# Two transformer blocks on one core: the low part of each weight half made in two GpSimd instructions of 512 elements instead of one of 1024

## The chip, the cores and the metric

The kernel runs on one core of one Trainium2 chip. Its time is the device time of one execution in microseconds (us). The engines of the core are TensorE (PE in the rows; its weight loads are PEld), VectorE (DVE), ScalarE (ACT), GpSimd (POOL) and SyncE (SP), which here only issues transfers.

## The reference, cut to what matters

Two blocks run one after the other on 256 tokens of width 2048, in float32. Nearly all of the work is the product of an activation with a large weight matrix:

```python
x = first_block(x, c, w_ada, ..., w_in, ..., w_out, ..., w_up, ..., w_down, final_norm_g)
return second_block(x, mem_2, ..., w_in_2, ..., w_xq_2, w_xk_2, w_xv_2, w_xo_2, ..., w_gate_2, w_up_2, w_down_2, final_norm_2)

# first_block
mod = jax.nn.silu(c) @ w_ada[l] + b_ada[l]            # 2048 -> 12288
h = rms_norm(x, norm_mix_g[l]) * (1.0 + scale_m) + shift_m
proj = h @ w_in[l]                                     # then block attention and a state space mixer
mix = jnp.concatenate([attn, ssm], axis=-1) @ w_out[l]
x = x + gate_m * mix
x = x + gate_f * conv_ffn(h, w_up[l], conv_ffn_w[l], conv_ffn_b[l], w_down[l])   # 2048 -> 11264 -> 2048

# second_block: neighbourhood and latent attention, attention on a memory, then
def swiglu(h, w_gate, w_up, w_down):
    return (jax.nn.silu(h @ w_gate) * (h @ w_up)) @ w_down
```

## The kernel before, in words

**Two parts of every weight.** TensorE takes operands of the type float32r. A float32 weight is therefore split in two: its high part `w_hi` is the weight cast to float32r, and its low part `w_lo` is the weight less that high part. The activation is split likewise into `a_hi` and `a_lo`. A product is three matmuls into the same sum: high by high (L1102), low activation by high weight (L1104), and high activation by low weight (L1106). Where the weights are the moving operand, the three stand at L1116, L1118 and L1120.

**The stream.** All weights pass in one fixed order (the list `STREAM`) as 442 tiles of 128 x 2048 elements, 1 MB each. A tile has two halves of 128 x 1024. A half `h` passes four engines:

- SyncE loads its tile into one of four slots of `raw` (`stream_tile`, L405). Before it overwrites a slot, it waits until the low parts of the old tile are made, since those read `raw`.
- ScalarE casts the half into `w_hi[h % 4]` (`hi`, L515). It first waits for `half_used`, which says that TensorE has finished half `h - 4`.
- GpSimd subtracts and writes `w_lo[h % 4]` (`low_part`, L481 to L485, the instruction at L484). It waits for `hi_ready` of the half and signals `lo_pool`. It does so for 882 of the 884 halves; the two halves of the tile `dt` are made by VectorE. GpSimd does nothing else but a few fills at the start.
- TensorE waits for `lo_pool` once ahead of a half (`wait_half`) and then runs its matmuls: 8 products of three matmuls of 256 columns (`half_T`), or 4 products of three of 512 columns (`half_N`, for the weights `xv`, the last third of `qkv` and a few others). Then it signals `half_used`.

So there are four slots of high and low parts: ScalarE and GpSimd can be up to four halves ahead of TensorE.

**Around the stream.** The stages come in this order: `xk`, `xv` (the keys and values of the memory for the second block, put first), `xs`, `dt`, `bz`, `qkv`, `wb`, `wa`, `up`, `down` for the first block, then `win2`, `uq`, `ukv`, `wa2`, `wb2`, `xq`, `xo`, `gu`, `down2` for the second. The heads of the attentions and of the mixer are worked between halves.

**The modulation.** The product with `w_ada` runs beside the stream on VectorE. 192 rows of 128 x 1024 are loaded into a ring of four slots, later two (`ada_row` in the SyncE program), and each is multiplied by an element of a vector and added to a sum (L1711; in the `up` stage L2144). Such an instruction reads two operands from on-chip memory. SyncE's queue holds tiles and rows in one order: `tiles_beside` puts about one row behind each half in the early stages. A row that waits for its slot (`ada_used`) holds back the tiles behind it.

**VectorE's other work** is the norms (L1792, L1801), the low parts of the activations (L1784, L1861, L2216), residuals, and the convolution behind `up` (L1875, L1880).

In every program, the order is that in which the code is written; no scheduler changes it.

Of the kernel before, what the change touches and what calls it, by code (L numbers as in the profile page):

```python
# [23 lines left out]
F32 = mybir.dt.float32  # L24
F32R = mybir.dt.float32r
I32 = mybir.dt.int32
ALU = mybir.AluOpType
# [11 lines left out]
HALF = TILE // 2  # L39
RAW = 4  # L40
SLOTS = 4
# [151 lines left out]
def block_program(nc, stream, ada, xT, memT, vecs, consts, onehot, relb, rpb, out, rel_dram,  # L193
                  rpb_dram, k_dram, v_dram):
    ctx = ExitStack()
    with ctx:
        def sb(name, shape, dt=F32):
            return ctx.enter_context(nc.sbuf_tensor(name, shape, dt))

        def sem(name):  # L200
            return ctx.enter_context(nc.semaphore(name))
# [3 lines left out]
        w_hi = sb("w_hi", [P, SLOTS, HALF], F32R)  # L205
        w_lo = sb("w_lo", [P, SLOTS, HALF], F32R)
# [111 lines left out]
        hi_ready, lo_dve, lo_pool = sem("hi_ready"), sem("lo_dve"), sem("lo_pool")  # L318
# [69 lines left out]
        def raw_half(h):  # L388

            return raw[:, h // 2 % RAW, h % 2 * HALF:(h % 2 + 1) * HALF]  # L390
# [86 lines left out]
        @block.gpsimd  # L477
        def _(pool):
            pool.memset(ones[:, :], 1.0).then_inc(ones_ready, 1)

            def low_part(h, i=None, step=0):  # L481

                pool.wait_ge(hi_ready, h + 1 if i is None else i * step + (h + 1))
                pool.tensor_tensor(w_lo[:, h % SLOTS], raw_half(h), w_hi[:, h % SLOTS].bitcast(F32),  # L484
                                   ALU.subtract).then_inc(lo_pool, 1)  # L485

            def low_parts(name, a, b):

                h0, period = H0[name], 16
                n = (b - a) // period  # L490
                if n >= 2:
                    with pool.Fori(0, n) as i:
                        for h in range(h0 + a, h0 + a + period):
                            if not ON_DVE[h]:
                                low_part(h, i, period)
                    a += n * period
                for h in range(h0 + a, h0 + b):
                    if not ON_DVE[h]:
                        low_part(h)

            for name, n in STREAM:
                low_parts(name, 0, 2 * n)
# [2145 lines left out]
```

## Time and profile before

| what | us |
|---|---|
| median of 3 runs | 3088.03 (3085.39 to 3088.13) |
| the profiled execution | 3092.41 |
| its span, first to last instruction | 3090.6 |
| TensorE busy (matmuls) | 2819.7 |
| GpSimd busy | 2240.9 |
| VectorE busy | 1189.6 |
| ScalarE busy | 1178.4 |

The span is the time between the first and the last instruction in the trace; 1.8 us of the profiled execution lie around it. Busy time counts an instruction from its start to its end in the records, waiting for a shared resource included. TensorE's matmuls overlap in the records, so that its busy time says when it has work rather than how fast it does it.

### The profile page before, as it was taken

The page shows a single profiled execution, that of the slowest core. Times are in us where ns is not written, and L with a number is a line of the kernel's source. Part 1 is how long each engine was busy: PE and PEld are TensorE (multiplying, and loading weights), DVE is VectorE, ACT ScalarE, POOL GpSimd, SP SyncE. Part 2 cuts the span into 40 slices and gives each one's busy share as a digit, 9 for nine tenths or more (in the row PEclk, how much of TensorE's full clock was granted, in tenths as well). Part 3 has the DMA queues.
Part 4 walks back from the last instruction along what each step waited for, and adds up shares of the span by engine and source line. Part 5 has one row for each costly group of instructions (what it writes and reads, how often), then busy time and mean ns, then how long its engine had stood idle before and what let it go on. Part 6 is the DMA issues. An engine that isn't in the chain of part 4 may idle for free.

```text
span 3090.6 us, 51906 instructions
## 1 busy us (share of the span) xinstructions
PE 2819.7 (91%) x21456; PEld 2730.9 (88%) x21456; DVE 1189.6 (38%) x1334; ACT 1178.4 (38%) x1349; POOL 2240.9 (73%) x887
## 2 busy tenths in 40 slices
PE   4688988786789999999999997999999999999997
PEld 4676987675679999999999996799999999999997
DVE  4787765543643544522233525361121000001233
ACT  2333332223233333333455434353354333333442
POOL 2679584443458889887888975476688888887885
PEclk8889898988889999999999999999999999999998
DMA  7877465544436666554444554253455455554542
GB/s 218 337 299 294 183 248 207 202 176 179 181 125 224 226 224 235 221 179 163 178 175 177 191 186 128 95 200 143 150 177 182 184 178 188 177 184 163 183 179 93
DMA packets 111622, 589.78 MB, mean 191 GB/s; under 512 B 23276, under 2 KB 25324, under 8 KB 54796
## 3 DMA queue, kind: packets, MB, share of 16 engines
q1 hardware_dynamic: 92736, 570.84, 50.6%
q10 hardware_dynamic: 18764, 17.20, 2.2%
q8 instruction: 90, 1.47, 0.2%
q14 instruction: 32, 0.26, 0.0%
HBM read 577.79 MB, written 10.21 MB: 190 GB/s over the span
## 4 chain that ended last, share of the span: by engine, by line
PE 41%; POOL 28%; issue 23%; DVE 5%; DMA 2%; ACT 1%; POOLq 0%; ACTq 0%; SPq 0%; DVEq 0%
POOL w_lo L484 28%; PE ps L1102 12%; PE ps L1104 12%; PE ps L1106 12%; DMA arena<-ada 2%; ACT w_hi L515 1%; DVE arena L1711 1%; PE ps L1116 0%; PE ps L1118 0%; PE ps L1120 0%; DVE work L1801 0%; PE ps L1567 0%; DVE work L1792 0%; PE ps L1161 0%; PE ps L1536 0%
## 5 line engine op out<-in xcount | busy, mean ns | idle before, releaser
L484 POOL TENSOR_TENSOR w_lo<-raw,w_hi 128x1024 fp32r<-128x1024 f32 x882 | 2240.5, 2558 | 816.0 <-ACT w_hi L515 814.3
L1102 PE MATMUL ps<-a_hi,w_hi 128*128 128x256 f32 x6512 | 1872.5, 288 | 122.6 <-POOL w_lo L484 43.9
L1104 PE MATMUL ps<-a_lo,w_hi 128*128 128x256 f32 x6512 | 1859.1, 285 | 0.0
L1106 PE MATMUL ps<-a_hi,w_lo 128*128 128x256 f32 x6512 | 1858.1, 285 | 0.0
L515 ACT CAST w_hi<-raw 128x1024 fp32r<-128x1024 f32 x884 | 919.7, 1047 | 1322.4 <-PE ps L1106 1169.2
L1102 PEld LDWEIGHTS ps<-a_hi,w_hi 128*128 128x128 f32 x6512 | 1268.5, 195 | 131.8 <-issue 57.1
L1104 PEld LDWEIGHTS ps<-a_lo,w_hi 128*128 128x128 f32 x6512 | 1268.2, 195 | 0.6
L1106 PEld LDWEIGHTS ps<-a_hi,w_lo 128*128 128x128 f32 x6512 | 1266.7, 195 | 0.0
L1711 DVE SCALAR_TENSOR_TENSOR arena<-arena,small 128x1024 f32<-128x1024 f32 x150 | 325.7, 2201 | 245.4 <-DMA arena<-ada 244.7
L1861 DVE TENSOR_TENSOR a_lo<-arena,a_hi 128x1024 fp32r<-128x1024 f32 x44 | 107.2, 2441 | 348.3 <-ACT a_hi L781 348.3
L2488 DVE TENSOR_TENSOR work<-ps,rstd 128x512 f32<-128x512 f32 x22 | 15.2, 692 | 430.4 <-PE ps L1106 430.4
L1875 DVE TENSOR_SCALAR work<-ps,vec 128x256 f32<-128x256 f32 x100 | 47.5, 539 | 239.5 <-PE ps L1106 239.5
L1116 PE MATMUL ps<-w_hi,a_hi 128*128 128x512 f32 x264 | 111.5, 422 | 5.4 <-POOL w_lo L484 5.3
L1118 PE MATMUL ps<-w_hi,a_lo 128*128 128x512 f32 x264 | 106.1, 402 | 0.0
L1120 PE MATMUL ps<-w_lo,a_hi 128*128 128x512 f32 x264 | 105.9, 401 | 0.0
L2144 DVE SCALAR_TENSOR_TENSOR arena<-arena,small 128x1024 f32<-128x1024 f32 x32 | 84.3, 2657 | 44.5 <-DMA arena<-ada 44.0
L1880 DVE SCALAR_TENSOR_TENSOR work<-ps,vec,work 128x255 f32<-128x255 f32 (+2 forms) x212 | 87.7, 476 | 5.5 <-DVE work L1875 2.4
L1116 PEld LDWEIGHTS ps<-w_hi,a_hi 128*128 128x128 f32 x264 | 51.9, 197 | 23.3 <-POOL w_lo L484 10.8
L1120 PEld LDWEIGHTS ps<-w_lo,a_hi 128*128 128x128 f32 x264 | 51.4, 195 | 11.7
L1118 PEld LDWEIGHTS ps<-w_hi,a_lo 128*128 128x128 f32 x264 | 51.8, 196 | 10.0
L2239 DVE TENSOR_TENSOR arena<-ps,rstd 128x1024 f32<-128x1024 f32 (+1 forms) x15 | 18.1, 1205 | 108.7 <-PE ps L1106 108.6
L2206 DVE TENSOR_REDUCE stage_v<-work 128x256 f32<-128x1024 f32 (+1 forms) x18 | 35.0, 1954 | 54.8 <-ACT work L818 54.8
(209 smaller groups left out, 1264.5 us busy)
## 6 DMA issues: line engine op xcount, KB each, us to landing
raw<-stream SPq DMA_DIRECT2D x442, 1024.0 KB, 4.8
arena<-ada SPq DMA_DIRECT2D x192, 512.0 KB, 5.7
arena<-memT SPq DMA_DIRECT2D x4, 512.0 KB, 7.8
res<-xT SPq DMA_DIRECT2D x1, 2048.0 KB, 23.9
rel_rows<-arena ACTq DMA_DIRECT2D x1, 2048.0 KB
k_spill<-arena ACTq DMA_DIRECT2D x4, 512.0 KB, 7.0
v_spill<-arena ACTq DMA_DIRECT2D x4, 512.0 KB, 3.3
work<-rel_rows ACTq DMA_DIRECT2D x16, 128.0 KB, 2.2
```

What stands on the lines that cost most here:

```text
L484: pool.tensor_tensor(w_lo[:, h % SLOTS], raw_half(h), w_hi[:, h % SLOTS].bitcast(F32), ALU.subtract).then_inc(lo_pool, 1)
L515: act.copy(w_hi[:, base % 4], raw[:, tile_slot, (base % 2) * HALF:(base % 2 + 1) * HALF]).then_inc(hi_ready, 1)
L1102: pe.matmul(o, w_hi[:, h % SLOTS, w], a_hi[:, c0 + k, :], start=first and k == 0 and f % 2 == 0, stop=False, skip_group_check=True)
L1104: pe.matmul(o, w_hi[:, h % SLOTS, w], a_lo[:, c0 + k, :], start=False, stop=False, skip_group_check=True)
L1106: mm = pe.matmul(o, w_lo[:, h % SLOTS, w], a_hi[:, c0 + k, :], start=False, stop=last and k == 1, skip_group_check=True)
L1116: pe.matmul(out2[:, t, 0:width], a_hi[:, c0 + k, a], w_hi[:, h % SLOTS, w], start=first and k == 0, stop=False, skip_group_check=True)
L1118: pe.matmul(out2[:, t, 0:width], a_lo[:, c0 + k, a], w_hi[:, h % SLOTS, w], start=False, stop=False, skip_group_check=True)
L1120: mm = pe.matmul(out2[:, t, 0:width], a_hi[:, c0 + k, a], w_lo[:, h % SLOTS, w], start=False, stop=last and k == 1, skip_group_check=True)
L1711: ins = dve.scalar_tensor_tensor(out=a, in0=ada_slot(n % ring), scalar=ck, in1=a, op0=ALU.mult, op1=ALU.add)
L1861: dve.tensor_tensor(a_lo[:, a:a + 4, :], hidden[:, 4 * quad:4 * quad + 4, :], a_hi[:, a:a + 4, :].bitcast(F32), ALU.subtract).then_inc(hl_ ...
L1880: ins = dve.scalar_tensor_tensor(out=dst[:, c, shift:S], in0=src[:, c, 0:S - shift], scalar=w(c, taps - 1 - shift), in1=dst[:, c, shift:S] ...
L2144: dve.scalar_tensor_tensor(out=a, in0=ada_slot(s % 2), scalar=small[:, bass.ds(i * 2 + (16 + s // 2), 1)], in1=a, op0=ALU.mult, op1=ALU.ad ...
```

## The change

For each half, GpSimd makes the low part in two instructions, of the first and of the last 512 elements of each partition. It waits once, ahead of the first, for `hi_ready`, and signals `lo_pool` once, behind the second. So each of TensorE's and SyncE's waits stands for the same event as before: the whole half is made. The number of elements is the same. There are 1764 such instructions in place of 882. No other engine's program is changed. In the changed file the lines behind the edit are numbered higher by 2.

```diff
             def low_part(h, i=None, step=0):
 
                 pool.wait_ge(hi_ready, h + 1 if i is None else i * step + (h + 1))
-                pool.tensor_tensor(w_lo[:, h % SLOTS], raw_half(h), w_hi[:, h % SLOTS].bitcast(F32),
-                                   ALU.subtract).then_inc(lo_pool, 1)
+                for cols in (slice(0, HALF // 2), slice(HALF // 2, HALF)):
+                    ins = pool.tensor_tensor(w_lo[:, h % SLOTS, cols], raw_half(h)[:, cols],
+                                             w_hi[:, h % SLOTS, cols].bitcast(F32), ALU.subtract)
+                ins.then_inc(lo_pool, 1)
```

## Rows read from the trace of the kernel before

**Rows 1.** The page: busy us (share of span) and instructions of each engine.

```profile
PE 2819.7 (91%) x21456; PEld 2730.9 (88%) x21456; DVE 1189.6 (38%) x1334; ACT 1178.4 (38%) x1349; POOL 2240.9 (73%) x887
```

**Rows 2.** Windows, whole core: start:end, length, busy (count) by engine, clock, DMA.

```profile
199.00:303.00 104.00, 97.97 (x419) 75.52 (x418) 85.18 (x38) 37.86 (x37) 99.93 (x33) 0.98 0.83 310
...
910.00:1419.00 509.00, 508.99 (x4231) 509.00 (x4231) 219.34 (x325) 194.64 (x198) 436.65 (x174) 1.00 0.58 211
...
2295.00:2804.00 509.00, 508.50 (x4232) 508.09 (x4230) 41.23 (x59) 200.32 (x204) 426.00 (x177) 1.00 0.51 182
```

**Rows 3.** Timeline of GpSimd: start us, us, what, [idle before <- releaser].

```profile
15.51 9.27 POOL L484 TENSOR_TENSOR w_lo<-raw,w_hi 128x1024 fp32r<-128x1024 f32 x4 [14.56 <-ACT w_hi L515]
...
2499.39 2.41 POOL L484 TENSOR_TENSOR w_lo<-raw,w_hi 128x1024 fp32r<-128x1024 f32 x1 [0.47 <-ACT w_hi L515]
2502.27 2.41 POOL L484 TENSOR_TENSOR w_lo<-raw,w_hi 128x1024 fp32r<-128x1024 f32 x1 [0.47 <-ACT w_hi L515]
```

**Rows 4.** Windows by 100 us, whole core (columns as in rows 2).

```profile
1000.00:1100.00 100.00, 100.00 (x836) 100.00 (x835) 48.60 (x68) 37.38 (x38) 89.25 (x36) 1.00 0.62 229
```

**Rows 5.** Timeline of GpSimd and VectorE around the stage xv.

```profile
194.81 99.33 POOL L484 TENSOR_TENSOR w_lo<-raw,w_hi 128x1024 fp32r<-128x1024 f32 x32 [0.48 <-ACT w_hi L515]
...
198.69 60.14 DVE L1711 SCALAR_TENSOR_TENSOR arena<-arena,small 128x1024 f32<-128x1024 f32 x18
```

**Rows 6.** Timeline of TensorE in xv, three matmuls of a product in a row.

```profile
202.62 0.39 PE L1116 MATMUL ps<-w_hi,a_hi 128*128 128x512 f32 x1
202.85 0.39 PE L1118 MATMUL ps<-w_hi,a_lo 128*128 128x512 f32 x1
203.08 0.39 PE L1120 MATMUL ps<-w_lo,a_hi 128*128 128x512 f32 x1
```

**Rows 7.** Chain of waits, 199 to 303 us: start us, us, what.

```profile
264.38 1.00 POOL w_lo L484
265.37 2.33 issue
267.71 1.00 POOL w_lo L484
```

**Rows 8.** Waits in the whole span: who <- whom: us, times, longest.

```profile
PEld ps L1102 <- POOL w_lo L484: 46.8, 13, 27.5
PE ps L1102 <- POOL w_lo L484: 43.9, 10, 27.3
```

**Rows 9.** Timeline of GpSimd at the start: its other instructions.

```profile
0.25 0.10 POOL L2638 MEMSET const-float32-0.0<- 128x1 f32 x1 [0.25 <-issue]
0.29 0.10 POOL L2638 MEMSET const-float32-1.0<- 128x1 f32 x1
...
0.75 0.20 POOL L479 MEMSET ones<- 128x128 f32 x1 [0.29 <-POOLq L2638]
```

**Rows 10.** Chain of waits in the whole span: start us, us, what.

```profile
298.55 7.52 DVE work L1801 x4
...
337.08 3.42 DVE arena L1711
...
403.44 3.14 DVE arena L1711
...
790.62 3.47 DVE arena L1711
```

**Rows 11.** Timeline of VectorE behind 296 us.

```profile
298.55 7.51 DVE L1801 TENSOR_SCALAR work<-work,mod 128x256 f32<-128x256 f32 x4
...
309.06 1.14 DVE L1801 TENSOR_SCALAR work<-work,mod 128x256 f32<-128x256 f32 x4
```

**Rows 12.** The page: chain that ended last, its largest shares by engine and line.

```profile
PE 41%; POOL 28%; issue 23%; DVE 5%; DMA 2%; ACT 1%; POOLq 0%; ACTq 0%; SPq 0%; DVEq 0%
POOL w_lo L484 28%; PE ps L1102 12%; PE ps L1104 12%; PE ps L1106 12%; DMA arena<-ada 2%; ACT w_hi L515 1%; DVE arena L1711 1%; PE ps L1116 0%; PE ps L1118 0%; PE ps L1120 0%; DVE work L1801 0%; PE ps L1567 0%; DVE work L1792 0%; PE ps L1161 0%; PE ps L1536 0%
```

**Rows 13.** The page: DMA issues, KB each, us to landing.

```profile
arena<-ada SPq DMA_DIRECT2D x192, 512.0 KB, 5.7
```

**Rows 14.** The page: groups; count | busy us, mean ns | idle before.

```profile
L1711 DVE SCALAR_TENSOR_TENSOR arena<-arena,small 128x1024 f32<-128x1024 f32 x150 | 325.7, 2201 | 245.4 <-DMA arena<-ada 244.7
```

## The prediction, on record before the changed kernel ran

> **What bounds the kernel now.** I read the engines' totals first [rows 1]: TensorE is busy for 91% of the span, GpSimd for 73%, the other two for 38%. That makes TensorE the usual bound and GpSimd the second engine. But the change touches GpSimd alone, and a share over the whole span says nothing of the stages in which GpSimd comes last. So I went through the stages by windows [rows 2].
>
> In `gu` (2295 to 2804 us) TensorE has work all the time, and 176 halves take 509 us, 2.89 us each. GpSimd makes a low part in 2.41 us and then idles for 0.47 us until ScalarE's next cast [rows 3], which itself waits for TensorE to free a slot. An instruction may grow by up to 0.47 us per half there at no cost. `up` (910 to 1419 us) has the same pitch. Its first part is tighter: GpSimd is busy for 89.25 us of 100 [rows 4], so the 34.7 halves of 2.88 us in it leave 10.75 / 34.7 = 0.31 us each.
>
> `xv` (199 to 303 us) is another case: GpSimd is busy for 99.93 of 104 us [rows 2], with 32 instructions on end in 99.33 us [rows 5], 3.10 us each. TensorE needs less: three matmuls start 0.23 us apart [rows 6], and a half has twelve, 2.76 us. The chain shows the same pitch of 3.34 us again and again, 1.00 on GpSimd's instruction and 2.33 on TensorE's issue behind it [rows 7]. GpSimd sets the time of this stage.
>
> Why does an instruction take 3.34 us there when four on end at the start take 9.27 us, 2.32 each [rows 3]? Beside it VectorE runs rows of the modulation, 18 on end in 60.14 us, also 3.34 us each [rows 5]. The two engines take turns: 2.30 us for GpSimd and 1.04 us for VectorE, one after the other. In the Trainium skill, "SBUF — State Buffer" (on-chip memory), the part on the shared port pair, VectorE with two inputs there and GpSimd exclude each other for a whole instruction; by that rule, the trace agrees, the turn and not the element is the grain, and halving GpSimd's instruction halves VectorE's wait for its turn without changing the sum of a turn of each.
>
> Outside `xv`, TensorE waits for a low part 10 times ahead of L1102, 43.9 us in all, of which 27.3 is one wait near the start [rows 8]. These are the places where work other than the stream held TensorE or ScalarE up, and the next halves are then made as fast as GpSimd can.
>
> **What the change does, part by part.**
>
> *It adds 882 instructions.* Each half still has 1024 elements per partition, so the added cost is what an instruction costs beyond its elements; call it X, when the next one is ready behind it. The trace has no 512-element subtraction, so X is bounded by rows. From below: the tiny fills of one element follow each other 0.04 us apart (0.25 to 0.29) [rows 9]. A gain in GpSimd's own work is excluded, since no element is saved. From above: such a fill takes 0.10 us from start to end [rows 9] and has one operand where the subtraction has three; three such parts are 0.30 us (an estimate). The fill of 128 elements takes 0.20 us, so its elements cost 0.10 and the rest is again 0.10. I take X = 0.15 us, between 0.10 and 0.20, since a two-input instruction has more to start and to drain than a fill, but part of that overlaps: the instruction behind an idle gap takes 2.41 us, those on end 2.32 each, so about 0.1 us of an instruction's cost is already hidden when one follows another [rows 3].
>
> The Trainium skill, "GPSIMD Engine Reference", section 3.1, has 4497 ns for a subtraction-like instruction of 2048 elements. With this trace's 2.41 us for 1024, a line through both has 0.32 us beyond the elements, 0.22 when they run on end; by it X would be 0.22 and the cost below 16 instead of 11 us.
>
> *In `xv`* GpSimd is the bound, and X is paid for each of about 32 halves: 32 x 0.15 = 4.8 us.
>
> *At the 10 waits outside `xv`* TensorE waits for the next low part and then runs close behind GpSimd. At most four halves are in the ring, and I charge four per wait: 10 x 4 x 0.15 = 6.0 us. Some waits expose only one half and some a longer catch-up, so this is a rough term.
>
> *In the long steady stages* (`up`, `down`, `win2`, `xo`, `gu`, `down2`) the idle time of 0.47 us per half, or 0.31 us in the first part of `up`, hides X. Cost 0. The cover is gone above X = 0.31: then about 150 halves of `up` pay the excess.
>
> *Semaphores.* TensorE and SyncE wait for the whole half as before, so nothing starts earlier for having the first 512 elements. Gain 0. SyncE's tile load waits for the low parts too, but loads up to eight halves ahead of TensorE. Cost 0 beyond the X counted.
>
> *VectorE gets its turn sooner.* A VectorE instruction that finds GpSimd on the shared memory waits up to 2.30 us now and up to 1.15 us after. This counts only where VectorE is last. The chain has four long places of that kind [rows 10]. Three are single modulation rows of 3.42, 3.14 and 3.47 us, against 1.04 us in its turn; each can lose 1.15 us, 3.4 in all. The fourth is the norm behind `xv`: four L1801 take 7.51 us at 298.55 and only 1.14 us at 309.06 with nothing in the way [rows 11]. It waited behind nearly three GpSimd instructions, 6.4 us; behind as many of half the length it would be 3.2 us. Together 6.6 us. GpSimd loses what VectorE takes, and TensorE needs both, so I count 5 us of it as gained.
>
> *Sum:* 4.8 + 6.0 - 5 = +6 us (5.8). The profiled execution took 3092.41 us (span 3090.6, 1.8 around it) and would become 3098. It was 4.4 us above the median of the runs, 3088.03, so for the runs I predict 3094.
>
> **Rivals.**
>
> *A. The instruction is dear.* If X is 0.30 us, `xv` costs 9.6 and the waits 12.0; less 5, that is +17: 3105 us. At 0.35 the `up` stage joins with 150 x 0.04 = 6 us, and the sum is 11.2 + 14 + 6 - 5 = +26: 3114 us. For it: the subtraction has two inputs and an output to set up. Against it: 0.10 us for the shortest fill.
>
> *B. The instruction is almost free, and VectorE gains nothing.* With X at 0.04, `xv` costs 1.3 and the waits 1.6 us; the turns of VectorE move work around without shortening the chain. +3: 3091 us, no change. For it: GpSimd and VectorE need the same sum of turns. Against it: the 6.4 us in front of L1801 stand in the chain.
>
> *C. The shorter turn wins: faster.* Place: the modulation rows beside the stream from 300 to 860 us. Transfers of such rows make 2% of the chain, 62 us [rows 12]; at 5.7 us to the landing of one [rows 13] these are about 11, and each is released by a VectorE row that gave its slot free. SyncE's queue holds the weight tiles behind these rows, so 1.15 us sooner per row would bring tiles sooner: 11 x 1.15 = 13 us, plus 3.2 at the norm, 16 in all. Half of it, 8, against a cost of 3 at X = 0.04 gives -5 to -6 us: 3082; all of it 3075. It decides when X is below about 0.1 us. Against it: VectorE mostly waits for the transfer itself, not for GpSimd.
>
> *D. The steady stages lose their cover* though X is small, because GpSimd now meets VectorE twice per half: each of the two instructions may have to give VectorE a turn of 1.04 us. In `up` VectorE is busy 48.6 of 100 us [rows 4], its waits for turns included, and its rows come once per four halves, so a second turn per half is rarely asked for. Would it cost 0.1 us per half, X would be 0.25 in effect and the sum 8 + 10 - 5 = +13: 3101. I count it with A.
>
> **How the numbers follow.** The forecast, X from 0.1 to 0.2 and some of the turns gained, has a chance of 0.45; its own range is 3088 to 3101. A and D together have 0.22, B has 0.15, C has 0.18. A change of less than 0.2%, 6.2 us, can't be told from none. The forecast lies on that line, so 0.22 of its chance is slower and 0.23 is the same. A and D are slower (0.22), B is the same (0.15), and of C 0.14 is faster and 0.04 is the same. Slower 0.44, same 0.42, faster 0.14. The range is 3080 to 3116: it leaves out C in full and X above 0.35 us.
>
> **What would show it.** In the changed profile GpSimd has twice as many subtractions. In `gu` two on end should take about 2.41 + 0.15 = 2.56 us, with the idle time per half down from 0.47 to 0.32 us and the stage still at 509 us. In `xv` the pitch of a half should be near 3.34 + 0.15 where rows run beside it, and the stage some 5 us longer. VectorE's L1711 should fall from 2.20 us on average [rows 14] towards 1.6, and the four L1801 from 7.5 towards 4.3 us. The prediction is wrong in its cost if the two instructions on end take 2.35 or 2.75 us, and in its gain if L1711 gets shorter while the stages up to 900 us stay as long as they were, or shrink by more than 6 us.

## The result and the profile after

The changed kernel takes 3109.25 us (3107.62 to 3110.53, 4 runs) against 3088.08: 21 us slower, ratio 1.007 with a 95% interval of 1.0053 to 1.0088. Run again beside the experiments, on another chip, it took 3105.81 us against 3090.33, ratio 1.0046 (1.0033 to 1.006). So the cost is 14 to 21 us; forecast were 6, with a range from 8 us less to 28 more.

The engines' totals of the changed kernel (busy us, share, instructions), as [rows 1]:

```profile
PE 2828.5 (91%) x21456; PEld 2738.1 (88%) x21456; DVE 1041.8 (34%) x1334; ACT 1182.2 (38%) x1349; POOL 2402.4 (77%) x1769
```

GpSimd is busy for 161.5 us more; 882 x 0.15 would be 132, and the rest fits more waiting for its turn. VectorE is busy for 148 us less with the same instructions: it waits less for its turn.

GpSimd's timeline, at the start and in `gu`, as [rows 3]:

```profile
15.57 9.84 POOL L485 TENSOR_TENSOR w_lo<-raw,w_hi 128x512 fp32r<-128x512 f32 x8 [14.61 <-ACT w_hi L517]
...
2502.97 2.56 POOL L485 TENSOR_TENSOR w_lo<-raw,w_hi 128x512 fp32r<-128x512 f32 x2 [0.32 <-ACT w_hi L517]
2505.86 2.56 POOL L485 TENSOR_TENSOR w_lo<-raw,w_hi 128x512 fp32r<-128x512 f32 x2 [0.33 <-ACT w_hi L517]
```

Four halves on end take 9.84 us instead of 9.27, and a half in `gu` 2.56 instead of 2.41, with an idle time of 0.32 instead of 0.47. The price of the second instruction is 0.14 to 0.15 us, as forecast.

The groups of VectorE's modulation rows and of the activation's low parts, as [rows 14] (L1713 is L1711 of before; L1863 was L1861, 2441 ns on average):

```profile
L1713 DVE SCALAR_TENSOR_TENSOR arena<-arena,small 128x1024 f32<-128x1024 f32 x150 | 258.5, 1745 | 321.2 <-DMA arena<-ada 320.9
L1863 DVE TENSOR_TENSOR a_lo<-arena,a_hi 128x1024 fp32r<-128x1024 f32 x44 | 71.1, 1619 | 390.5 <-ACT a_hi L783 390.5
```

Where did the time go? This table has the end of each stage, read from the timeline as the end of the matmul that signals the stage's last half, in us, and how much later than before each profile is at that point. "Again" is the second run of the changed kernel; the last four columns are kernels of the experiments below:

| end of | before | changed | again | 16, 1008 | 1008, 16 | only xk | wait per piece |
|---|---|---|---|---|---|---|---|
| xk | 199.4 | -8.5 | -9.2 | -10.3 | -9.0 | -9.3 | -8.9 |
| xv | 302.4 | -1.3 | -3.8 | -2.6 | -3.0 | -7.7 | -4.8 |
| wa | 888.3 | +3.9 | 0.0 | -5.2 | +1.3 | -11.5 | +3.7 |
| up | 1418.6 | +6.6 | +2.7 | -4.7 | +6.0 | -8.8 | +3.6 |
| down | 1686.8 | +11.2 | +7.2 | -2.8 | +8.4 | -8.2 | +4.0 |
| win2 | 1890.2 | +16.7 | +12.3 | -1.1 | +10.2 | -8.1 | +6.6 |
| xo | 2294.9 | +17.7 | +14.0 | -0.3 | +14.6 | -7.1 | +3.6 |
| down2 | 3065.3 | +17.8 | +14.0 | -0.5 | +14.6 | -7.2 | +3.6 |

Each column is a single execution. That of the cut 16, 1008 was the fastest of its 11 (3091.89 us, median 3098.29), so its column is some 6 us too good as a whole; single stages can be compared. `gu` and `down2`, 770 us, lose nothing. `xk` gains 9 us, and what lies between loses more than forecast. Waits between 100 and 200 us, first of the kernel before, then of the changed one (who waited for whom: us, times, longest):

```profile
POOL w_lo L484 <- ACT w_hi L515: 29.6, 13, 17.1
...
PE ps L1186 <- DVE arena L1711: 7.8, 1, 7.8
```

```profile
POOL w_lo L485 <- ACT w_hi L517: 8.2, 2, 5.0
DVE arena L1713 <- DMA arena<-ada: 30.0, 13, 8.1
```

In `xk` TensorE stood for 7.8 us waiting for the 32 rows of the first modulation sum. With shorter turns VectorE has them ready in time: the changed kernel's list has no such wait. Then `xv` takes 110 us instead of 103 (108.5 in the second run). Not all of this is the price: with two pieces in `xk` alone, `xv` takes 104.5.

### The profile page after: what moved, and what is told of

Its sections match the earlier page's. It is cut to its first block, busy times and chain, and to the rows that moved or that the text cites. A ratio compares the mean times of both kernels' runs of the same rounds, so it can differ in the third digit from the quotient of the medians.

```text
span 3108.4 us, 52788 instructions
## 1 busy us (share of the span) xinstructions
PE 2828.5 (91%) x21456; PEld 2738.1 (88%) x21456; DVE 1041.8 (34%) x1334; ACT 1182.2 (38%) x1349; POOL 2402.4 (77%) x1769
## 4 chain that ended last, share of the span: by engine, by line
PE 39%; POOL 35%; issue 18%; DVE 4%; DMA 2%; ACT 1%; POOLq 0%; ACTq 0%; SPq 0%; DVEq 0%
POOL w_lo L485 35%; PE ps L1104 12%; PE ps L1106 11%; PE ps L1108 11%; DMA arena<-ada 2%; PE ps L1118 1%; PE ps L1120 1%; PE ps L1122 1%; PE ps L1569 0%; ACT w_hi L517 0%; PE ps L1425 0%; DVE rstd L2275 0%; PE ps L1538 0%; DVE arena L1713 0%; PE ps L1537 0%
## 5 line engine op out<-in xcount | busy, mean ns | idle before, releaser
L485 POOL TENSOR_TENSOR w_lo<-raw,w_hi 128x512 fp32r<-128x512 f32 x1764 | 2402.0, 1393 | 672.5 <-ACT w_hi L517 669.2
L1713 DVE SCALAR_TENSOR_TENSOR arena<-arena,small 128x1024 f32<-128x1024 f32 x150 | 258.5, 1745 | 321.2 <-DMA arena<-ada 320.9
L1863 DVE TENSOR_TENSOR a_lo<-arena,a_hi 128x1024 fp32r<-128x1024 f32 x44 | 71.1, 1619 | 390.5 <-ACT a_hi L783 390.5
L2146 DVE SCALAR_TENSOR_TENSOR arena<-arena,small 128x1024 f32<-128x1024 f32 x32 | 63.9, 2018 | 71.7 <-DMA arena<-ada 71.7
L764 ACT ACTIVATE work<-work 128x512 f32<-128x512 f32 x22 | 13.9, 633 | 106.8 <-DVE work L1882 106.8
```

Source lines behind the costliest of these rows:

```text
L485: ins = pool.tensor_tensor(w_lo[:, h % SLOTS, cols], raw_half(h)[:, cols], w_hi[:, h % SLOTS, cols].bitcast(F32), ALU.subtract)
L1713: ins = dve.scalar_tensor_tensor(out=a, in0=ada_slot(n % ring), scalar=ck, in1=a, op0=ALU.mult, op1=ALU.add)
L1863: dve.tensor_tensor(a_lo[:, a:a + 4, :], hidden[:, 4 * quad:4 * quad + 4, :], a_hi[:, a:a + 4, :].bitcast(F32), ALU.subtract).then_inc(hl_ ...
L2146: dve.scalar_tensor_tensor(out=a, in0=ada_slot(s % 2), scalar=small[:, bass.ds(i * 2 + (16 + s // 2), 1)], in1=a, op0=ALU.mult, op1=ALU.ad ...
```

## The experiments

Each ran beside the kernel before on one chip, and every ratio is to that. They ran in three groups on three chips, so kernels of different groups are compared by their ratios.

### Where the half is cut

```diff
-                for cols in (slice(0, HALF // 2), slice(HALF // 2, HALF)):
+                for cols in (slice(0, 16), slice(16, HALF)):
```

> Two instructions per half as in the changed kernel, cut into the first 16 elements and the other 1008. The price theory says that the 21 us come from the fixed cost of a second instruction alone (0.15 us, as in the changed profile, 2.56 against 2.41 us): it doesn't matter where the cut is, so about 3109 us. The turn theory says that part of the 21 us is VectorE taking the shared memory port between the two instructions of a half, which puts the end of the half off by about 1 us where GpSimd is last. An instruction of VectorE that becomes ready while GpSimd works nearly always falls into the 1008 elements and gets its turn behind the half, as in the kernel before: 3094 to 3101 us.

Measured: 3098.29 against 3089.56 us, ratio 1.0025 (1.0016 to 1.0034).

```diff
+                for cols in (slice(0, HALF - 16), slice(HALF - 16, HALF)):
```

> The same two instructions in the other order, 1008 elements and then 16. Price theory: about 3109 us, and the same as the cut at 16. Turn theory: VectorE gets its turn ahead of the last 16 elements nearly each time that it is ready, so every collision puts the half off by a whole turn: 3109 to 3120 us, and at least 8 us more than the cut at 16.

Measured: 3104.83 us, 1.0046 (1.0033 to 1.006), 6.5 us more than the cut at 16, on the same chip. The order of the two pieces matters, though instructions, elements and price are the same: a half has 2.55 or 2.56 us in `gu` in all three kernels. The turn theory named the sign and the first number; of the second, and of the distance (at least 8), it missed the size. By the ends of the stages in the two profiles, the distance arises mostly in `xs` (a loss of 4.2 us against a gain of 1.2; the changed kernel gains 0.8 there) and in `up` (4.7 against 0.5). The mechanism is plainest in `down`, where VectorE makes a low part of the activation every fourth half; GpSimd and VectorE at the cut 16, 1008:

```profile
1450.30 2.56 POOL L485 TENSOR_TENSOR w_lo<-raw,w_hi 128x16 fp32r<-128x16 f32 x2 [0.32 <-ACT w_hi L517]
1453.18 8.32 POOL L485 TENSOR_TENSOR w_lo<-raw,w_hi 128x16 fp32r<-128x16 f32 x6 [0.32 <-ACT w_hi L517]
...
1451.21 2.74 DVE L1863 TENSOR_TENSOR a_lo<-arena,a_hi 128x1024 fp32r<-128x1024 f32 x1 [8.78 <-ACT a_hi L783]
```

and in the changed kernel:

```profile
1450.32 11.19 POOL L485 TENSOR_TENSOR w_lo<-raw,w_hi 128x512 fp32r<-128x512 f32 x8 [0.33 <-ACT w_hi L517]
...
1451.23 1.47 DVE L1863 TENSOR_TENSOR a_lo<-arena,a_hi 128x1024 fp32r<-128x1024 f32 x1 [13.23 <-ACT a_hi L783]
```

At the cut 16, 1008 the first half ends undisturbed after 2.56 us, and VectorE waits for it. In the changed kernel VectorE gets in between the two pieces and finishes after 1.47 us, so that the first half is the one that ends late. The four halves together are made in 11.2 us in both; only which one is put off differs. Here this costs nothing: from the 8th to the 60th half of `down` no column of the table moves. It costs where TensorE is close behind GpSimd. In `up`, VectorE's modulation row at the same place of a period of 16 halves, at the cut 16, 1008:

```profile
1102.30 3.42 DVE L2146 SCALAR_TENSOR_TENSOR arena<-arena,small 128x1024 f32<-128x1024 f32 x1 [2.41 <-DMA arena<-ada]
```

and in the changed kernel, with TensorE's wait between 1112 and 1126 us:

```profile
1111.76 2.20 DVE L2146 SCALAR_TENSOR_TENSOR arena<-arena,small 128x1024 f32<-128x1024 f32 x1 [1.28 <-DMA arena<-ada]
```

```profile
PEld ps L1104 <- POOL w_lo L485: 0.3, 1, 0.3
```

The first row waits for a whole half. The second gets its turn after the first 512 elements, the half's signal comes at 1115.11, and TensorE stands 0.3 us for it. The changed kernel loses 0.4 us in each of seven such periods of `up`, in both its profiles. The cut 1008, 16 loses 0.4 as well, and the cut 16, 1008 0.05.

### Which stages

Two pieces only in some stages (`stages` stands for the names):

```diff
+                name = [n for n in T0 if H0[n] <= h][-1]
+                for cols in ((slice(0, HALF // 2), slice(HALF // 2, HALF)) if name in stages else (slice(0, HALF),)):
```

> Two instructions of 512 only in the stages xk to wa (the first 890 us), one of 1024 in all later ones. My sum on record had 4.8 us for xv and most of the 10 waits here, less 5 for VectorE: about +4, 3092 us. The changed profile has the end of wa 3.9 us later than before. If the first stages carry most of the 21 us: above 3100.

Measured: 3091.7 us, 1.0004 (0.9995 to 1.0013), as the sum had it. By its profile this is a gain of 8.7 us in `xk` and a loss of as much behind it.

> Two instructions of 512 only in the stages up to xo (890 to 2295 us of the kernel before), one of 1024 elsewhere. The sum on record had about nothing in up and down, and the rest of the 10 waits: +2, 3090 us. The changed profile loses 13.8 us between the ends of wa and xo, which would be 3102 us. Price theory: 0.15 us per half where GpSimd is last, of 384 halves, at most 58. Turn theory: the loss is in down, win2 and wb2, where VectorE makes low parts of activations and norms.

Measured: 3099.11 us, 1.0031 (1.0019 to 1.0043). More than the 2 us of the sum, less than the 14 of the changed kernel's profile.

> Two instructions only in gu and down2, one elsewhere. The idle time of 0.47 us per half hides 0.15 us: no change, -1 to +2 us. The two other partial kernels gave +1 and +10 of the 21 us. If costs just add, this one would have to bring 10 us; the changed profile has only 0.1 us there between the ends of xo and down2, so I expect that they don't add, or that the whole is less than 21.

Measured: 3090.39 against 3090.33 us, 0.9998 (0.9989 to 1.0007). The parts add to 10 to 12 us, which fits the second run of the changed kernel (14 us by the ratio 1.0046) within the intervals and not the first. The net cost lies between `up` and `xo`; up to `wa` gain and loss cancel; and the cover in `gu` is real.

> The changed kernel once more, beside the others on one chip, to narrow its own interval: 3109 us, ratio 1.005 to 1.009.

Measured: 3105.81 us, 1.0046 (1.0033 to 1.006).

### Without the modulation rows

VectorE works 16 instead of 1024 elements of each row after the first of a sum; the rest of the sum is left out, so the result is not that of the reference. The same is done at L2144 for the rows in `up`.

```diff
-                    ins = dve.scalar_tensor_tensor(out=a, in0=ada_slot(n % ring), scalar=ck, in1=a,
+                    ins = dve.scalar_tensor_tensor(out=a[:, 0:16], in0=ada_slot(n % ring)[:, 0:16], scalar=ck, in1=a[:, 0:16],
```

> The kernel before, with each row of the modulation after the first of a sum worked on 16 of its 1024 elements (the rest of the sum is left out); all loads and waits stay. VectorE then needs hardly any turn on the shared port for these rows. GpSimd's pitch in xv should be 2.3 us instead of 3.3, so that TensorE or the loads bound xv, and the wait of TensorE for the first modulation sum (7.8 us) should shrink: 15 to 40 us less than before.

Measured: 3034.5 against 3090.33 us, 56 less; the rows cost more than I had thought. Their own work is gone here as well as their turns.

> The same on the changed kernel. Its distance from the run with short rows and one instruction per half tells how much of the 21 us needs the rows. If the price of 0.15 us alone is paid wherever a low part is last: still above 12 us. If the cost needs VectorE's turns next to GpSimd's: xv and up lose nothing, down and win2 keep part of theirs, 4 to 9 us between the two.

Measured: 3051.26 us (3043.89 to 3057.45, 4 runs), 17 more than with one instruction. So the cost does not need the rows' full length, and the expectation of 4 to 9 us fell. In `xv` it came true: GpSimd's timeline there with one and with two instructions per half:

```profile
219.79 2.40 POOL L484 TENSOR_TENSOR w_lo<-raw,w_hi 128x1024 fp32r<-128x1024 f32 x1 [0.32 <-ACT w_hi L515]
222.51 2.40 POOL L484 TENSOR_TENSOR w_lo<-raw,w_hi 128x1024 fp32r<-128x1024 f32 x1 [0.32 <-ACT w_hi L515]
```

```profile
221.41 2.55 POOL L485 TENSOR_TENSOR w_lo<-raw,w_hi 128x512 fp32r<-128x512 f32 x2 [0.17 <-ACT w_hi L517]
224.13 2.55 POOL L485 TENSOR_TENSOR w_lo<-raw,w_hi 128x512 fp32r<-128x512 f32 x2 [0.17 <-ACT w_hi L517]
```

Both have a pitch of 2.72 us, set by TensorE, and 0.15 us goes from the idle time. But in `up` the second kernel loses 7.4 us, in two jumps of 3.0 and 4.5. Ahead of the second, VectorE's row of 16 elements, GpSimd, and ScalarE's step that waits for the convolution behind the row:

```profile
1106.41 8.80 DVE L2146 SCALAR_TENSOR_TENSOR arena<-arena,small 128x16 f32<-128x16 f32 x1 [7.52 <-DMA arena<-ada]
...
1095.05 20.12 POOL L485 TENSOR_TENSOR w_lo<-raw,w_hi 128x512 fp32r<-128x512 f32 x16 [1.76 <-ACT w_hi L517]
1122.30 2.50 POOL L485 TENSOR_TENSOR w_lo<-raw,w_hi 128x512 fp32r<-128x512 f32 x2 [7.13 <-ACT w_hi L517]
...
1120.66 0.63 ACT L764 ACTIVATE work<-work 128x512 f32<-128x512 f32 x1 [8.94 <-DVE work L1882]
```

A row of 16 elements took 8.80 us. It ends as GpSimd runs out of work at 1115.17: some six pieces of GpSimd went by without VectorE getting a turn. The convolution behind it on VectorE comes late, ScalarE waits 8.94 us for it, the casts are queued behind that, GpSimd idles for 7.13 us, and TensorE then waits 2.7 us for a low part. Taking turns, on which my prediction rested, is not always what happens.

### One instruction off the shared port

The longest such case of the changed kernel is in `win2`. VectorE and GpSimd:

```profile
1733.71 10.11 DVE L2275 TENSOR_TENSOR rstd<-rstd 128x256 f32<-128x256 f32 x1
...
1716.00 27.53 POOL L485 TENSOR_TENSOR w_lo<-raw,w_hi 128x512 fp32r<-128x512 f32 x22 [2.19 <-ACT w_hi L517]
1748.94 25.64 POOL L485 TENSOR_TENSOR w_lo<-raw,w_hi 128x512 fp32r<-128x512 f32 x20 [5.41 <-ACT w_hi L517]
```

Before, the same product of 256 elements took 1.78 us. Now it ends only when GpSimd has stopped, at 1743.5. ScalarE waits 6.5 us for what follows on VectorE, its casts are queued behind, and so GpSimd idles for 5.41 us. Measured by the ends of the halves, TensorE falls back there by 4.0 us in one profile of the changed kernel and by 3.7 in the other. The experiment lets the product read one operand from PSUM:

```diff
-            root(v2, u2, row_b)
-            dve.tensor_tensor(row_a, row_b, row_c, ALU.mult).then_inc(row_ready, 1)
+            root(v2, u2, row_b, u1)    # the last step of the root writes u1, in PSUM
+            dve.tensor_tensor(row_a, u1, row_c, ALU.mult).then_inc(row_ready, 1)
```

> The changed kernel, with one VectorE instruction in win2 taken off the shared port: the product of two norm rows (L2275, 128x256) reads one of them from PSUM. In the changed profile this instruction takes 10.1 us, since GpSimd's 512-element instructions pass it by until GpSimd runs dry, against 1.8 us in the profile before, and the stage win2 is about 4 us late from there on. Passed-over theory: the instruction takes 0.4 us, the 4 us come back, about 3102 us (4 less than the changed kernel in its second run, 3106). Price theory: the 4 us are GpSimd's longer halves, nothing comes back, 3106 us.

Measured: 3104.74 against 3088.94 us, 1.0051 (1.0039 to 1.0064). The time shows nothing that came back, but each ratio has 4 us of doubt to either side, so it hardly decides between the two theories. The trace does:

```profile
1727.68 0.42 DVE L2276 TENSOR_TENSOR rstd<-ps,rstd 128x256 f32<-128x256 f32 x1
1728.13 1.22 DVE L2242 TENSOR_TENSOR arena<-ps,rstd 128x1024 f32<-128x1024 f32 x1
1729.28 24.35 DVE L2282 TENSOR_TENSOR res<-res,rstd 128x1024 f32<-128x1024 f32 x1
...
1709.91 42.64 POOL L485 TENSOR_TENSOR w_lo<-raw,w_hi 128x512 fp32r<-128x512 f32 x34 [2.17 <-ACT w_hi L517]
1760.52 10.36 POOL L485 TENSOR_TENSOR w_lo<-raw,w_hi 128x512 fp32r<-128x512 f32 x8 [7.97 <-ACT w_hi L517]
```

The product takes 0.42 us. By the ends of the halves, this profile's lead over the changed kernel's second one grows there from 2.0 to 6.6 us. Then the next instruction with two inputs in on-chip memory is passed by, for 24.35 us, until GpSimd's 34 pieces on end are over at 1752.6. Eight halves later the lead is 2.2 us again. So being passed by costs these 4 us, and freeing one instruction handed the cost to the next. At the end of this profile the lead is 5.2 us: it grows behind `win2`, where the code is the same, and this execution (3101.19 us) was among the fastest of six.

### A wait per piece

TensorE waits for each piece by itself, and each piece signals:

```diff
-                ins.then_inc(lo_pool, 1)
+                    ins.then_inc(lo_pool, 1)
...
+                pe.wait_ge(lo_pool, n * 2 - 1)    # ahead of the first 512 elements
...
+                    if k:
+                        wait_rest()                # ahead of the last 512
```

SyncE's wait counts both signals, so it stands for the same event as before.

> The changed kernel, with a signal behind each of the two instructions and a wait of TensorE for each: the first 512 elements are used 1.3 us sooner. Where TensorE has caught up with GpSimd once and then runs behind it, each such place gets about 1.2 us shorter. With 5 to 10 such places 6 to 12 us less than the changed kernel: 3094 to 3100 us. If TensorE loses its lead in another way (by slots that come free late), no change: 3106.

Measured: 3093.79 us (3085.63 to 3111.38, 12 runs), 1.0021 (1.0006 to 1.0036): by the ratios 8 us less than the changed kernel in its second run, as expected. Its column in the table tells where. From the end of `wa` to the end of `down2` it loses nothing on balance, where the changed kernel loses 14; `up` and the two places in `down` with norm work lose nothing. There the cost is TensorE waiting for the second piece where it has caught up. Between `xk` and `wa` it loses 12.6 us, no less than the changed kernel, so that part has another reason; in `xv`, where GpSimd sets the time, it is in part the price itself. It is not faster than the kernel before.

### Two pieces only in xk

> Two instructions only in the first stage, xk. In the changed profile TensorE no longer waits 7.8 us for the first modulation sum there, and xk ends 8.5 us sooner; xv, bound by GpSimd at 0.15 us more per half, gave nearly all of it back. With one instruction per half in xv, GpSimd's lead of about one and a half halves (some 5 us) should stay: 3084 to 3086 us, faster than before. If the gain is lost anyway, because GpSimd and not TensorE sets the end of xv: 3089.

Measured: 3081.94 against 3088.94 us, 0.9978 (0.9969 to 0.9987): 7 us faster than the kernel before, somewhat more than expected. The profile keeps 7.7 us at the end of `xv` and 7.2 at the end of `down2`.

> Candidate for a kernel better than both: two instructions only in xk, and the norm row product in win2 off the shared port. 1.4 us less than two_in_xk, since the product takes 1.8 us with one instruction per half and would take 0.4: 3083 us.

Measured: 3083.87 us, 0.9978 (0.9969 to 0.9987). The product off the shared port adds nothing that can be told; with instructions of 1024 elements there were 1.4 us to win by the expectation, less than the interval.

## Why the prediction was right in sign and price, and too low in size

The sum was -5 for shorter turns, 4.8 in `xv`, 6.0 at ten waits and nothing in the steady stages. The second run of the changed kernel has, by the table: -9.2 in `xk`, +5.4 in `xv`, +3.8 from there to the end of `wa`, +2.7 in `up`, +4.5 in `down`, +5.1 in `win2`, +1.7 up to the end of `xo`, 0 in `gu` and `down2`: 14.0.

The result lies inside my range, but for a reason that the runs refute: I had drawn it up to +28 for rival A, an instruction that costs 0.30 us or more, and it costs 0.15. That it was wide enough is luck. Rival D, in which GpSimd meets VectorE twice per half, comes nearest: it had +13, and I thought it too rare to count.

**The bound in each stage: right.** `xv` was GpSimd's, `gu` was covered (ratio 0.9998 for `gu` and `down2` alone), and short rows freed `xv` of the cost.

**X: right.** 0.15 us taken, 0.14 to 0.15 measured, wherever the cut is. The estimate of 0.22, from a line through the Trainium skill's 4497 ns ("GPSIMD Engine Reference", section 3.1), was too high.

**xv: 4.8 us forecast, 5.4 and 7.2 in the two profiles.** Right in kind. But 1.5 us of it comes even with one instruction per half here, when `xk` has two; why was not measured.

**The gain of shorter turns: 5 forecast, 9 found, at another place.** I looked for it at single long rows in the chain. The four L1801 did fall, from 7.51 to 3.22 us. But most of it is the wait for the first modulation sum, 7.8 us, at which I had not looked. It is a shorter turn that wins, as in rival C, but some 140 us earlier than C put it, and by the sum being ready sooner rather than by tiles that come sooner. All of it was gone by the end of `wa` in the second run of the changed kernel.

**Cover in the steady stages: right for the price, wrong for the turns in `up`.** I set 0.31 us of idle time against 0.15 and charged 0. `up` loses 0.4 us each 16 halves, in seven of its eleven periods: in the chain of waits, the same piece recurs after 46.08 us before and 46.5 in the changed kernel.

```profile
1053.49 3.86 issue
...
1099.57 3.87 issue
...
1145.65 3.87 issue
```

```profile
1116.33 3.15 POOL w_lo L485 x3
...
1162.81 3.16 POOL w_lo L485 x3
...
1209.31 3.15 POOL w_lo L485 x3
```

The price alone was covered: the cut 16, 1008 pays it too and loses 0.05 us a period, and with a wait per piece the loss is nil. What costs is a row that gets its turn ahead of the second piece of a half for which TensorE is about to wait. Rows fall on a few halves in each period, so idle time on average says little about them. It is the stage that rival D named and my sum charged nothing for.

**The 10 waits: 6.0 us forecast for the whole kernel, too small.** From the end of `up` to `xo` alone the second run of the changed kernel loses 11.3 us. Of this, 3.7 is the passed-over instruction in `win2`, a term that the sum lacked. Two places in `down`, where norm work is put between halves, lose 2.1 us each in both its profiles, but 0.9 each in those of the other cuts and of the kernel with two pieces from `up` to `xo`, which has the same code there. With a wait per piece they lose nothing. So what such a place costs depends on how the engines meet, beyond the price. How the rest splits between the price and VectorE's turns was not measured, nor what makes up the 3.8 us between `xv` and the end of `wa`.

The price of an instruction was sized well. The step that failed is the exposure: I charged the price to a few waits (6.0 us, and 0 in the steady stages, against 17.8 us lost behind `xv` in the second run) and let VectorE's turns only help. A turn between the two pieces puts off the half that TensorE waits for, and a long row of pieces can keep VectorE out.

## What to carry to other kernels

Two engines that exclude each other per instruction make the length of an instruction a scheduling choice. Shorten it only in the stretch where the other engine is the one that is waited for (here: 7 us gained from 32 halves, 14 to 21 lost from all 882). When an instruction is cut, let the consumer wait for the pieces, or else the half gets later by everything that slips in between (here this took back 8 of 14 us). Idle time averaged over a window covers a price that is paid evenly, as in `gu`, but not a turn that falls on a few halves; look at a period of the loop.

## What the runs showed of the hardware that was not expected

- **VectorE can be passed by.** With 512-element pieces on end on GpSimd, a VectorE instruction with two inputs in on-chip memory took 10.1 us (256 elements, in five of the profiles at the same place; 7.5 us there at the cut 1008, 16), 8.8 us (16 elements) and 24.35 us, each but the one of 7.5 us ending when GpSimd ran dry. With 1024-element instructions the longest single one took 5.35 us (a row of 16 elements). The Trainium skill, "SBUF — State Buffer", section "SBUF: two separate sides", says that whichever starts first holds the pair for the whole instruction and the other fully blocks. The turns of 3.34 us agree with that. It doesn't tell who is next, and here it was the same engine up to some 18 times. What decides it stays open.
- **The second instruction costs the same for 16 elements as for 512**, 0.14 to 0.15 us: four halves at the start take 9.84 to 9.86 us with all three cuts.
